# Moving the region of the activations by 32 bytes in SBUF, in a two-layer decoder trunk

## The reference

```python
h = rms_norm(x, norm_mix[0]); p = h @ w_in_ab            # 1024 -> 2816 columns
x = x + concat(gmlp(p), dilated_attention(p)) @ w_out_ab
x = x + swiglu(rms_norm(x, norm_ffn[0]), ffn_w_gate, ffn_w_up, ffn_w_down)   # 2816 wide
h = rms_norm(x, norm_mix[1]); p = h @ w_in_cd            # 1024 -> 3072 columns
x = x + concat(moba_attention(p), short_conv(p)) @ w_out_cd
# top 2 of 8 experts, each a SwiGLU of width 3584
x = x + sum(gate[e] * swiglu(rms_norm(x, norm_ffn[1]), wg[e], wu[e], wd[e]) for e in range(8))
```

## Time and profile before

| | |
|---|---|
| time, median of 3 runs | 1409.17 us (1409.05 to 1409.74) |
| the profiled execution, first to last instruction | 1407.9 us; its own time is not among the numbers given, so the 1.3 us between this span and the median stand for what lies around it |
| TensorE matmuls busy | 1394.9 us, 99% |
| weight loads busy | 1150.2 us, 82% |
| VectorE busy | 1196.3 us, 85% |
| ScalarE busy | 1025.8 us, 73% |
| bytes read from HBM | 425.09 MB, 307 GB/s over the span |

### The profile page before, as it was taken

One profiled execution on the slowest core, in us unless ns is written; L12 is line 12 of the kernel. 1 busy time (PEld: TensorE's weight loads), 2 busy tenths in 40 slices (PEclk: granted clock), 3 DMA queues, 4 the chain that ended last, 5 costly groups with the idle time before them and its releaser, 6 DMA issues.

```text
span 1407.9 us, 20276 instructions
## 1 busy us (share of the span) xinstructions
PE 1394.9 (99%) x6985; PEld 1150.2 (82%) x6985; DVE 1196.3 (85%) x1517; ACT 1025.8 (73%) x1262; POOL 58.9 (4%) x67
## 2 busy tenths in 40 slices
PE   9999999999999999999999999999999999999998
PEld 7778999988888788888888888888888888888886
DVE  4876555568859999999999999999999999999998
ACT  5666444466758778778777877887787788778776
POOL 0020000000410000000000000000000000000000
PEclk9999999999999999999999999999999999999999
DMA  9943443733749999999999999999999999999980
GB/s 347 345 160 136 180 150 120 259 101 131 260 160 362 354 364 342 394 367 368 365 371 371 349 388 363 377 360 379 363 347 389 365 359 375 376 352 361 387 301 30
DMA packets 183760, 430.28 MB, mean 306 GB/s; under 512 B 5449, under 2 KB 13301, under 8 KB 183712
## 3 DMA queue, kind: packets, MB, share of 16 engines
q1 hardware_dynamic: 181408, 423.86, 81.7%
q0 software_dynamic: 2304, 5.78, 2.1%
HBM read 425.09 MB, written 7.34 MB: 307 GB/s over the span
## 4 chain that ended last, share of the span: by engine, by line
PE 94%; DVE 4%; ACT 1%; issue 1%; DVEq 0%; ACTq 0%
PE psum L720 30%; PE psum L722 29%; PE psum L721 29%; PE psum L1307 2%; DVE w_lo L390 1%; PE psum L1288 0%; PE psum L752 0%; DVE act_lo L1874 0%; PE psum L1151 0%; PE psum L853 0%; DVE probs L2072 0%; PE psum L994 0%; PE psum L885 0%; DVE rope_tmp L459 0%; DVE p_qk L461 0%
## 5 line engine op out<-in xcount | busy, mean ns | idle before, releaser
L408 DVE TENSOR_TENSOR w_lo<-raw_ring,w_hi 128x1024 fp32r<-128x1024 f32 x674 | 814.2, 1224 | 68.5 <-ACT w_hi L403 55.5
L403 ACT ACTIVATE w_hi<-raw_ring 128x1024 fp32r<-128x1024 f32 x675 | 714.8, 1062 | 191.9 <-PE psum L722 190.4
L720 PE MATMUL psum<-w_hi,xg_hi 128*128 128x512 f32 x896 | 357.9, 399 | 0.9 <-DVE w_lo L408 0.8
L722 PE MATMUL psum<-w_hi,xg_lo 128*128 128x512 f32 x896 | 353.7, 395 | 0.0
L721 PE MATMUL psum<-w_lo,xg_hi 128*128 128x512 f32 x896 | 353.6, 395 | 0.0
L390 DVE TENSOR_TENSOR w_lo<-raw_ring,w_hi 128x1024 fp32r<-128x1024 f32 x124 | 151.4, 1228 | 82.1 <-ACT w_hi L382 81.2
L382 ACT ACTIVATE w_hi<-raw_ring 128x1024 fp32r<-128x1024 f32 x124 | 130.2, 1058 | 98.9 <-PE psum L722 98.5
L722 PEld LDWEIGHTS psum<-w_hi,xg_lo 128*128 128x128 f32 x896 | 168.0, 187 | 40.8
L720 PEld LDWEIGHTS psum<-w_hi,xg_hi 128*128 128x128 f32 x896 | 168.0, 188 | 39.9 <-issue 1.2
L721 PEld LDWEIGHTS psum<-w_lo,xg_hi 128*128 128x128 f32 x896 | 168.2, 188 | 38.8
L720 PE MATMUL psum<-w_hi,moe_hT_hi 128*128 128x512 f32 x448 | 178.4, 398 | 0.0
(11 more groups left out here) (272 smaller groups left out, 1251.1 us busy)
## 6 DMA issues: line engine op xcount, KB each, us to landing
raw_ring<-in_moe_w_gate SPq DMA_DIRECT2D x56, 2048.0 KB, 9.7
raw_ring<-in_moe_w_up SPq DMA_DIRECT2D x56, 2048.0 KB, 10.0
raw_ring<-in_moe_w_down SPq DMA_DIRECT2D x56, 2048.0 KB, 9.9
raw_ring<-in_ffn_w_gate SPq DMA_DIRECT2D x5, 2048.0 KB, 7.8
raw_ring<-in_ffn_w_up SPq DMA_DIRECT2D x5, 2048.0 KB, 9.1
raw_ring<-in_ffn_w_down SPq DMA_DIRECT2D x5, 2048.0 KB, 10.3
raw_ring<-in_w_in_ab SPq DMA_DIRECT2D x4, 2048.0 KB, 16.4
raw_ring<-in_w_in_cd SPq DMA_DIRECT2D x4, 2048.0 KB, 8.1
```

Source lines behind the costliest of these rows:

```text
L403: act.activation(wh[:, v % SPLITS, :], moe_raw(i, q), ACT.Copy).then_inc(hi_ready, 1)
L408: dve.tensor_tensor(wl[:, v % SPLITS, :], moe_raw(i, q), wh[:, v % SPLITS, :].bitcast(F32), ALU.subtract).then_inc(lo_ready, 1)
L720: pe.matmul(out_, sh, mh_, start=start, stop=False)
L722: return pe.matmul(out_, sl, mh_, start=False, stop=stop)
```

## The change

The region begins 32 bytes later, and everything that is laid from `R0` or `R1` goes with it. `conv_y`, which was given relative to `R0`, keeps its place. Nothing else is changed: the same instructions in the same order, with other addresses.

```diff
+PHASE = 32
...
         row_scale = at("row_scale", [2, SEQ], F32, place[0])
         ws_t = keep("gmlp_wT", [GG, P])
-        R0 = place[0]
+        R0 = place[0] + PHASE
         act_hi = at("act_hi", [KD, SEQ], F32R, R0)
         act_lo = at("act_lo", [KD, SEQ], F32R, R0 + 8192)
         R1 = R0 + 16384
...
-        conv_y = at("conv_y", [2, SEQ], F32, R0 - 6144)
+        conv_y = at("conv_y", [2, SEQ], F32, place[0] - 6144)
```

## The result

The changed kernel takes 1384.03 us (median of 4 runs, 1383.98 to 1384.11) against 1409.41 us (1409.05 to 1409.74): the ratio is 0.9821, 95% interval 0.9807 to 0.9834. It is 25.4 us, 1.8%, faster. I had forecast 1407.8 us, no measurable difference, in a range from 1400 to 1417 us.

The account below looks back on a forecast made before the run. TensorE was taken to bound the kernel, by the distance between matmul starts. Term 1's -1.4 us, with the other terms 0, took 1409.17 to 1407.8 us, no measurable change; the range was 1400 to 1417 us.

Parts of the forecast that it names:

- The frame: Whole kernel: TensorE bounds it, terms are count x difference in distance; 1 ns on 512-column matmuls is 5.0 us.
- Term 4: ScalarE and VectorE: split passes keep 1062 and 1224 ns, other changes lie beside TensorE; taken as 0.
- Step 2: 5064 matmuls with activations stationary: fixed price at most 3 periods, 1.25 ns; taken as 0, lower bound -6.3 us.
- second witness: Transposes with stationary operand on or off a multiple of 64: eight take 1.03 us either way, so no offset price.
- Step 3: Both operands at the same place modulo 64: streams might clash, but last products show 230 ns each; taken as 0.
- Term 1: 1008 matmuls with activations moving: moving operand comes onto a multiple of 64, saving 1.4 ns each, -1.4 us.
- The slower rival: 5064 matmuls with activations stationary: stationary operand on a multiple of 64 costs 1.4 ns, +7.1 us, 1416.3 us; chance 0.20.
- the large gain: 512-column matmuls: 20 ns excess is a clash of one operand on, one off, and vanishes; floor about 1322 us; chance 0.08.
- the quarter: Within the large gain: a quarter of the 87 us down to the floor, giving 1387 us.

Follow-up runs that it names:

- the bursts: Kernels doing only 48-matmul bursts, other engines idle, operand places and widths varied; 512 columns: 226.7 ns at equal places modulo 256, 233.4 ns 32 bytes apart.

## Why the prediction was wrong

*The frame held.* The kernel is bound by the distance of matmuls, the term is count x difference, and one ns on 512 columns is worth 5 us: 5.8 to 5.9 ns by the table above made the gain. Term 4 held too: ScalarE's and VectorE's split passes take 1063 and 1224 ns after, as before.

*Step 2 failed, and it is the one that mattered.* It took any price of the stationary side to be the same for 256 and 512 columns, and from the two distances (280.5 and 560 periods) concluded that it was at most 3 periods. It was 16, 6.7 ns (560 to 544 periods), for 512 columns, while 256 columns lost 7 periods (116.9 to 120.0 ns). At relation 0 the excess is 32 periods for 256 and 32 for 512 columns; at 224 it is 24 and 48. Two points always lie on a line, and the line through zero was an accident: the widths in between (34.3 at 288, 32.2 at 384) don't lie on it. The transposes that I called as a second witness are bound by the load, as the bursts of 128, 192 and 224 columns seem to be with 111.4 to 112 ns whatever the width, and such a stream showed no difference at any relation tried. I had noted that limit and still let them count.

*Step 3 looked at the right thing and dismissed it.* The last products had relation 0 before the change, as all have now. I read 230 ns from two distances and called it "not more than 233.4 ns". In the trace the four starts lie at 1402.69, 1402.92, 1403.15 and 1403.39 us, 231 ns apart in the mean. The same four are 232 ns apart after the change, in a trace whose long streams run at 226.7 ns: a stream at relation 0 reaches its pace only after some nine matmuls, so four of them could not have settled it. They should have kept the case of a clash open, and not have closed it. I asked only whether a common place could be worse, not whether it could be better.

*Term 1 had the wrong sign.* I put the 1.4 ns between the earlier trace rows down to the moving operand. It is the difference between relation 224 and 32 at 256 columns, and the change brought both to 0, the slowest: +1.6 us on 1008 matmuls instead of -1.4 us. The slower rival read the same 1.4 ns as a price of the stationary operand and was wrong for the same reason; both gave to one operand what belongs to the pair.

*Of the rivals*, the large gain came nearest: a clash of two reads that goes away. It had a chance of 0.08, and its point of 1387 us is near the time. That is luck, since nothing stood behind the quarter that gave this point, and its picture was wrong in size: of the 20 ns over 213.3 ns a third goes, and 13.3 ns stay at the best place found. It is also not a matter of one operand on and one off modulo 64: relation 64 has both on and runs at 233.4 ns. The objection I raised against it, that the excess grows with the columns though the load doesn't, was the failed argument of step 2. I had also set against it that by the Trainium skill (page "TensorE: Matmul & The Clock Gate", section "Step-by-step: what each phase is for") weight loads and moving operands use two independent read ports. Here the measurement decides: in float32r the relation of the two addresses changes the pace by 6.7 ns, and in bf16 by nothing that shows. Whether the ports themselves get in each other's way, no run here can tell. The limit of VectorE was not reached; 939 - 891 = 48 us of slack are left.

## What to carry to other kernels

In a stream of float32r matmuls that reloads its stationary operand each time, the places of the two operands modulo 256 bytes, relative to each other, are worth up to 3% of the stream (226.7 against 233.4 ns at 512 columns). For 512 moving columns lay both at the same place modulo 256, at multiples of 32 bytes, and the low parts of a split product too, since one of three pairs out of place takes back most of the gain. For each other width try other relations in steps of 32 bytes, since the best place for 256 columns (224) costs 233.4 ns at 512. Read the price from distances over 30 or more matmuls in one undisturbed stream, compare like widths only, and where no row has the new combination, one kernel of bursts gives the whole table.

## What the runs showed of the hardware

- float32r matmuls of 512 columns never followed each other in steady state at less than 226.6 ns, 31.8 periods over their columns, with other engines idle; bf16 ones do so at 215.9 ns, 6 periods over.
- A load of 32 stationary columns beside 512 moving ones gave a slower stream (230.3 to 240.3 ns over four places) than one of 128 columns at relation 0.
- At relation 0 a stream of 512 columns in the kernel needs some nine matmuls after each restart to reach 226.7 ns, and starts at about 233.
- A float32r weight load of 128 columns is shown with 188 ns, a bf16 one with 97 to 98 ns.
- Between the multiples of 32 bytes the same places (`ds` = 16) gave 226.6 ns in one burst and 233.1 ns in another, in another kernel of bursts with a different burst before it, so something besides these places has a part in it.
